# Other places in SBUF for the woven activations, and another order of a block's three products, in a hybrid decoder layer on one core

## What is computed

```
h = rmsnorm(x); z = h @ w_in                  # queries | latent kv | rope key | pooling channels | 2 gates
merged = sigmoid(gA) * (attention(z) @ w_attn_out) + sigmoid(gB) * (pooling(z) @ w_pool_out)
x = x + merged @ w_o
h = rmsnorm(x); z = h @ w_up                  # 2 x 5632 columns: gate half a, value half v
hid = silu(conv3(a)) * v                      # causal convolution of width 3 over time
x = x + hid @ w_down                          # then a final rmsnorm
```

## Time and profile before

| | us |
|---|---|
| median of 3 runs | 1941.05 (1939.59 to 1941.77) |
| the profiled execution | 1940.27 |
| its span (first to last instruction) | 1938.5 |
| PE busy | 1923.4 (99%), 13412 matmul records |
| DVE busy | 1089.9 (56%) |
| ACT busy | 759.3 (39%) |
| granted TensorE clock, mean | 0.998 of full (2.4 GHz) |

### The profile page before, as it was taken

One profiled execution on the slowest core, in us unless ns is written; L12 is line 12 of the kernel. 1 busy time (PEld: TensorE's weight loads), 2 busy tenths in 40 slices (PEclk: granted clock), 3 DMA queues, 4 the chain that ended last, 5 costly groups with the idle time before them and its releaser, 6 DMA issues.

```text
span 1938.5 us, 34193 instructions
## 1 busy us (share of the span) xinstructions
PE 1923.4 (99%) x13412; PEld 1905.2 (98%) x13412; DVE 1089.9 (56%) x1506; ACT 759.3 (39%) x846; POOL 96.2 (5%) x252
## 2 busy tenths in 40 slices
PE   9999999999999999999999999999999999999997
PEld 8999999999999999999999999999999999999997
DVE  6865344434345774455556565655656556565656
ACT  5456542332257643333343333332323333333334
POOL 1002000000000241000000000000000000000000
PEclk9999999999999999999999999999999999999999
DMA  7444444444443687454444344434344444344443
GB/s 255 152 152 179 151 152 152 151 151 152 151 172 138 211 309 259 174 206 151 150 160 144 141 165 140 164 139 164 138 165 154 150 154 151 136 168 137 167 138 122
DMA packets 60042, 318.18 MB, mean 164 GB/s; under 512 B 6674, under 2 KB 6994, under 8 KB 27346
## 3 DMA queue, kind: packets, MB, share of 16 engines
q1 hardware_dynamic: 59330, 313.15, 45.6%
q10 hardware_dynamic: 656, 4.27, 0.5%
HBM read 313.08 MB, written 4.32 MB: 164 GB/s over the span
## 4 chain that ended last, share of the span: by engine, by line
PE 94%; DVE 2%; ACT 1%; DMA 1%; issue 1%; SPq 0%; POOL 0%; DVEq 0%; POOLq 0%
PE ps L1656 94%; ACT w_hi L592 0%; DMA w_raw<-in_cache_t 0%; DVE keys_lo L1035 0%; DMA xT<-in_x 0%; PE ps L1973 0%; DMA c_raw<-in_cache 0%; DVE y_gain L1035 0%; DVE w_lo L1035 0%; POOL k_rope_all L558 0%; ACT sm L844 0%; DVE sm L1382 0%; SPq L433 0%; SPq L417 0%; PE ps L1923 0%
## 5 line engine op out<-in xcount | busy, mean ns | idle before, releaser
L1035 DVE TENSOR_TENSOR w_lo<-w_raw,w_hi 128x2048 fp32r<-128x2048 f32 (+1 forms) x251 | 571.0, 2276 | 433.7 <-ACT w_hi L592 433.7
L592 ACT ACTIVATE w_hi<-w_raw 128x2048 fp32r<-128x2048 f32 (+2 forms) x253 | 478.2, 1890 | 594.7 <-PE ps L1656 586.4
L1656 PE MATMUL ps<-h,w_hi 128*128 128x320 f32 x2816 | 590.4, 307 | 0.0
L1656 PEld LDWEIGHTS ps<-h,w_hi 128*128 128x128 f32 x2816 | 462.8, 188 | 0.2
L1656 PE MATMUL ps<-h,w_lo 128*128 128x320 f32 x1408 | 407.9, 307 | 1.3 <-DVE w_lo L1035 1.3
L1656 PE MATMUL ps<-h_hi,w_hi 128*128 128x320 f32 x1104 | 337.4, 309 | 0.0
L1656 PE MATMUL ps<-h_lo,w_hi 128*128 128x320 f32 x1104 | 332.9, 305 | 0.2 <-DVE h_lo L1127 0.2
L1656 PE MATMUL ps<-hid,w_hi 128*128 128x320 f32 x1426 | 308.8, 306 | 0.0
L1656 PE MATMUL ps<-h_hi,w_lo 128*128 128x320 f32 x1088 | 300.2, 307 | 0.0
L1656 PEld LDWEIGHTS ps<-h,w_lo 128*128 128x128 f32 x1408 | 258.5, 188 | 1.8 <-DVE w_lo L1035 1.8
L1656 PEld LDWEIGHTS ps<-hid,w_hi 128*128 128x128 f32 x1426 | 237.3, 188 | 0.0
(11 more groups left out here) (251 smaller groups left out, 2097.9 us busy)
## 6 DMA issues: line engine op xcount, KB each, us to landing
w_raw<-in_slabs SPq DMA_DIRECT2D x252, 1024.0 KB, 4.8
w_raw<-in_cache_t SPq DMA_DIRECT2D x64, 288.0 KB, 4.2
c_raw<-in_cache SPq DMA_DIRECT2D x56, 256.0 KB, 4.6
w_whole<-in_slabs SPq DMA_DIRECT2D x4, 1024.0 KB, 7.4
x_again<-in_x ACTq DMA_DIRECT2D x1, 2560.0 KB, 9.6
c_last<-in_cache SPq DMA_DIRECT2D x8, 256.0 KB, 4.4
xT<-in_x SPq DMA_DIRECT2D x3, 640.0 KB, 8.8
w_raw<-in_slabs SPq DMA_DIRECT2D x3, 512.0 KB, 7.8
```

Of the source, the lines that this page charges most:

```text
L592: return nc.scalar.activation(out, in_, ACT.Copy)
L1035: return nc.vector.tensor_tensor(out, a, b, op)
L1656: return nc.tensor.matmul(out, a, b, start=start, stop=stop, **kw)
```

## The change

It moves data and instructions; none is added and the arithmetic is the same.

- The lanes: hi from lane 0 to 2, lo from lane 1 to 0, the unsplit number from lane 2 to 1.
- The woven tensors (`h2`, `x1`, `hid`, `hid32`) begin 64 bytes further on. `sq`, `x_again`, `m32`, `y_gain` and `aext` move by 64 with them; `c_hi` and `c_lo` go from 64 to 320 bytes past `ch_reg`.
- In `slab`, w_hi x lo of block n comes right behind w_hi x hi of block n, and the w_lo product last. The same order is set in the down-projection.
- In chunks 1 to 10 `lag` is 0: each block's three products stand together, and PE waits for both halves at the slab's start. In chunk 0 slabs 4 and 5 get lag 16 as slabs 0 to 3 have; slabs 6 and 7 keep 2.

```
+HI_LANE, LO_LANE, OWN_LANE = 2, 0, 1
+WOVEN_AT = 64
...
-        c_hi = sb("c_hi", [P, RT, NP], F32R, at=ch_reg + 64)
+        c_hi = sb("c_hi", [P, RT, NP], F32R, at=ch_reg + 320)
...
-        h2 = sb("h2", [P, KD, T // 4, LANES, 4], F32R, at=r1)
-        h2_hi, h2_lo = h2[:, :, :, 0, :], h2[:, :, :, 1, :]
-        hid = sb("hid", [P, FPC, T // 4, LANES, 4], F32R, at=a_reg)
+        h2 = sb("h2", [P, KD, T // 4, LANES, 4], F32R, at=r1 + WOVEN_AT)
+        h2_hi, h2_lo = h2[:, :, :, HI_LANE, :], h2[:, :, :, LO_LANE, :]
+        hid = sb("hid", [P, FPC, T // 4, LANES, 4], F32R, at=a_reg + WOVEN_AT)
...
+                if lag == 0:
+                    pe.wait_ge(lo_ready, g + (1 - whole_before))
...
                             mm(out, w(w_hi[s]), hi, first, False)
-                        if n == step and not per_out:
+                            mm(out, w(w_hi[s]), lo, False, False)
+                        if n == step > 0 and not per_out:
                             pe.wait_ge(lo_ready, g + (1 - whole_before))
                         if n >= step:
-                            out_of_low, _, end, w_of_low, hi_of_low, _ = part[n - step]
-                            last = mm(out_of_low, w_of_low(w_lo[s]), hi_of_low, False, end)
-                        if n < len(part):
-                            mm(out, w(w_hi[s]), lo, False, False)
+                            out, _, end, w, hi, lo = part[n - step]
+                            last = mm(out, w(w_lo[s]), hi, False, end)
...
-                         lag=KD if first_chunk and l < 4 else 2)
+                         lag=0 if not first_chunk else KD if l < 6 else 2)
...
                         mm(out, blk(w_hi[s], w), hid_hi[:, k, :, :], k == 0, False)
-                        mm(out, blk(w_lo[s], w), hid_hi[:, k, :, :], False, False)
-                        last = mm(out, blk(w_hi[s], w), hid_lo[:, k, :, :], False, k == FPC - 1)
+                        mm(out, blk(w_hi[s], w), hid_lo[:, k, :, :], False, False)
+                        last = mm(out, blk(w_lo[s], w), hid_hi[:, k, :, :], False, k == FPC - 1)
```

More of the change, by code:

```diff
@@ L192, in program @@
         o_hi = sb("o_hi", [P, H, T], F32R, at=qn_reg)
-        x1 = sb("x1", [P, KD, T // 4, LANES, 4], at=r1)[:, :, :, 2, :]
-        sq = sb("sq", [P, KD, T], at=ol_reg)
+        x1 = sb("x1", [P, KD, T // 4, LANES, 4], at=r1 + WOVEN_AT)[:, :, :, OWN_LANE, :]
+        sq = sb("sq", [P, KD, T], at=ol_reg + WOVEN_AT)
         p_hi = sb("p_hi", [P, PT_, T], F32R, at=ol_reg)
         p_lo = sb("p_lo", [P, PT_, T], F32R, at=ol_reg + TB // 2)
-        x_again = sb("x_again", [P, KD, T], at=ol_reg)
+        x_again = sb("x_again", [P, KD, T], at=ol_reg + WOVEN_AT)
         c32_reg = region(RT * T * 4)
@@ L205, in program @@
         k_stack = sb("k_stack", [P, 2, NP], F32R)
-        c_hi = sb("c_hi", [P, RT, NP], F32R, at=ch_reg + 64)
-        c_lo = sb("c_lo", [P, RT, NP], F32R, at=ch_reg + 64 + RT * NP * 4)
-        m32 = sb("m32", [P, 2, T], at=ch_reg)
+        c_hi = sb("c_hi", [P, RT, NP], F32R, at=ch_reg + 320)
+        c_lo = sb("c_lo", [P, RT, NP], F32R, at=ch_reg + 320 + RT * NP * 4)
+        m32 = sb("m32", [P, 2, T], at=ch_reg + WOVEN_AT)
         mt = sb("m_tmp", [P, 2, T], at=ch_reg + 4096)
@@ L221, in program @@
         q_rope_hi = sb("q_rope_hi", [P, RT, NP], F32R, at=left)
-        h2 = sb("h2", [P, KD, T // 4, LANES, 4], F32R, at=r1)
-        h2_hi, h2_lo = h2[:, :, :, 0, :], h2[:, :, :, 1, :]
-        hid = sb("hid", [P, FPC, T // 4, LANES, 4], F32R, at=a_reg)
-        hid_hi, hid_lo = hid[:, :, :, 0, :], hid[:, :, :, 1, :]
-        hid32 = sb("hid32", [P, FPC, T // 4, LANES, 4], at=a_reg)[:, :, :, 2, :]
-        aext = sb("aext", [P, 2, CEXT], at=a_reg + FPC * LANES * T * 4)
+        h2 = sb("h2", [P, KD, T // 4, LANES, 4], F32R, at=r1 + WOVEN_AT)
+        h2_hi, h2_lo = h2[:, :, :, HI_LANE, :], h2[:, :, :, LO_LANE, :]
+        hid = sb("hid", [P, FPC, T // 4, LANES, 4], F32R, at=a_reg + WOVEN_AT)
+        hid_hi, hid_lo = hid[:, :, :, HI_LANE, :], hid[:, :, :, LO_LANE, :]
+        hid32 = sb("hid32", [P, FPC, T // 4, LANES, 4], at=a_reg + WOVEN_AT)[:, :, :, OWN_LANE, :]
+        aext = sb("aext", [P, 2, CEXT], at=a_reg + WOVEN_AT + FPC * LANES * T * 4)
         cv = sb("cv", [P, 3, CEXT], at=b_reg + 4096)
@@ L232, in program @@
         cstate = sb("cstate", [P, FT, 1 + NB, CW - 1], at=b_reg + 12288)
-        yg = sb("y_gain", [P, KD, T], at=ch_reg)
+        yg = sb("y_gain", [P, KD, T], at=ch_reg + WOVEN_AT)
         by_token = sb("rstd_by_token", [P, 5, 3], at=norm_reg)
```

## The result

The change makes the kernel slower: 1946.11 us median (1944.66 to 1947.05, 8 runs) against 1940.82 (1938.67 to 1941.77, 8 runs), a ratio of 1.0031 with a 95% interval of 1.0021 to 1.0040. The profiled execution has a span of 1945.2 us, before 1938.5.

A forecast was written before the change was run, and what follows sets the result against it. PE's matmul pace times count was taken as the bound; gains of 10.1 us (chunks 1 to 9), 2.4 (last chunk), 1.5 and 1.4 (first chunk), 0 (dense groups), together 15.4, gave 1926 us, range 1918 to 1948.

The forecast's parts named there:

- What bounds the kernel: Whole kernel: the matrix engine, PE, is busy 99%, so time is matmul count times start interval, plus a few waits.
- Part 1: Woven FFN matmuls: the new lanes and 64-byte shift cut the interval from 144.1 to 140 to 141 ns, slab 6.92 to 6.72 us.
- the half rival: Woven matmuls: only half the stall goes, 142 ns, slab 6.82 us, odd slabs still wait; 1931 us, chance 0.20.
- The inference from the latent keys: Latent-key matmuls, activations 64 bytes past their region's start, show no stall; so woven matmuls shifted likewise should lose theirs.
- Part 2: Low product last in each block: costed at nothing for the dense groups, within 1 us either way.
- Part 3: No lead in loop slabs: odd slabs wait for w_lo, a pair costs 13.75 us; chunks 1 to 9 gain 10.1 us.
- Part 4: First chunk, slabs 4 and 5 with 32 w_hi products first: slab 5's 1.52 us of idle time and refill goes.
- Slower, by the order: Woven slabs: reads of highs while w_hi loads stall most, 147 ns a matmul; 1958 us, chance 0.20.

## Why the prediction was wrong

The forecast was 1926 and faster; it came out slower, inside the stated range but on the other side.

- **What bounds the kernel** held: PE's pace times its count, and nothing else that moved by more than 2 us.
- **Part 1, the places.** "I take 140 to 141" is the first term that failed. The best pace that any kernel here had is 142.2 ns, the half rival's. The inference from the latent keys, that the 64 bytes take the stall away, does not hold: the 64 bytes with the old lanes give 145.2 ns, the lanes without the 64 bytes 145.3, and both with the old order 145.5. Only place and order together give 142.2. The pages of the Trainium skill named in the prediction would have all of these equal. In the Trainium skill, "TensorE: Matmul & The Clock Gate", section "Back-to-back issue gap", gives N / 2.4 + 2.5 for a matmul by itself, and says that pairs of weight load and matmul depart from it. For 320 columns it makes an estimate of 135.8 ns; the traces, all of them of pairs, have 142.2 to 146.7. By the prediction's own rows, too, the floor was 141 ns and not 140: 303 less the 162 of latency.
- **Part 2, the low product last.** For the dense groups the cost of nothing stands: their means are 309, 303 and 306 ns before, and 303, 309 and 306 after (the highs and the lows have changed places). The first matmul of the FFN came at 1006.6 to 1008.3 us in the twelve traces with this dense code, before at 1007.44, so the +0.69 of the table is within what the traces differ by. For the woven slabs the edit was judged by the pool map, whose activations are contiguous. At the old woven places the new order costs 12 us with a lead of two.
- **Part 3, no lead.** The chain was sized right. w_lo came at the very moment that slab 3 could have started, and PE lost 0.23 us at it (0.15 until the first matmul, 0.08 until the second) where 0.06 + 0.10 were forecast. **The step that failed is the price of that wait**: 13.75 us for a pair, as if a wait cost its own length and the next pair were like the last. It was felt once, for 0.23 us, and never again, since it turned the pace from 142.2 to 145.6 ns and then the low halves came 0.36 us or more ahead. That is 1.92 us a chunk, 18.8 us to the end of the kernel. The forecast for the loop, 81.88 us a chunk, was met to 0.04 us by the kernel with the waits moved, but by another sum: 12 slabs at 6.83, and no pair held up.
- **Part 4, the first chunk** was right: slab 5 starts at 1043.65 (within the 0.2 us of 1043 only when the FFN's later start is taken off), goes through 32 products without idle time, and its first w_lo product comes at 1048.38. The chunk gained 1.90 us where 2.9 were forecast: 1.5 for the wait, as forecast, and 0.4 by the pace in place of 1.4.
- **The rivals.** "Slower, by the order" has the result at the lower edge of its band (from 1945; its own time, 1958, is 12 us off), but its mechanism is not what happened: the same order runs at 142.2 ns in every chunk of the loop in the kernel with both waits late. At the old places the pace is the rival's, 146.7 ns; whether its mechanism makes it so was not tested. The half case had the pace (142) and the waits, and 1931 us; it lacked what the first wait does to the pace. None of the rivals had a pace that depends on what went before.

What is open is why these patterns exist. In the changed kernel the starts repeat to 1 ns, every block of three products in the better pattern and every two blocks in the slower one, whatever DVE, ACT and the DMAs do beside them. In the kernel before, with its lead, they have no such short period. That the reads of activations and of weights meet in some order, and that this order is carried from one matmul to the next, is a guess; no run here looked into it, and place and order were varied only at the points described above.

## What to carry to other kernels

When PE is the bound, look at its pace in several stretches and not as one mean: two paces for the same instructions on the same addresses say that history decides, and then a wait is priced by the pace behind it and not by its length. Put each wait directly ahead of the first instruction that needs it, since two products' worth of room (0.28 us) was worth 18.8 us here. Price place and order together, at the very layout that is to be used: alone they cost 8 us (place) and 12 us (order), both together gained 6 with a lead of two, and 12 with no lead and no gap.

## What was not expected of the hardware

- The interval of like matmuls has several self-sustaining patterns: 142.2 and 145.6 ns for the same code and data places. A gap of 0.09, 0.15 or 4.5 us (the last with a fall of the clock) turned the first into the second, which then lasted to the end, some 800 us, where no slab had a lead. A slab with a lead of two blocks, and the next, brought the first back; with a lead of one in every slab the two took turns slab by slab. Not every gap turns it: one of 0.07 us did so in one chunk and not in another of the same kernel.
- The mean interval of the woven matmuls depends on the lane order, on a shift of 64 bytes and on the order of the products, each in an interplay with the others: 142.2, 144.1, 145.2, 145.3, 145.5, 145.6, 146.7 ns.
- The same kernel had two times from run to run, at the same granted clock of 0.998: 1933 to 1935 or 1945 to 1946 us, where a wait had 0.06 us of room in the one run with a trace.
- After 4.4 us of idle time PE's granted clock was at the lower level, 1.2 GHz, from 1088.70 to 1094.90 us, with matmuls 267 ns apart. That added 3.0 us to the gap's 4.5, and 2.6 us in the kernel with the lead.
